# First projection unit in two halves, its first norm's weights fetched ahead of it, in a hybrid transformer layer on one core

## The reference

```python
h = rmsnorm(x, norm_mix[i])
proj = h @ w_in[i]                      # 1024 x 3584
rq, rk, rv, rg, dq, dk, dv = jnp.split(proj, ...)
mix = jnp.concatenate([retention(rq, rk, rv, rg), diff_attention(dq, dk, dv, ...)], axis=-1)
x = x + mix @ w_out[i]
h = rmsnorm(x, norm_ffn[i])
x = x + hierarchical_moe(h, ...)        # 16 experts, two per token
gate = jax.nn.sigmoid(rmsnorm(x, norm_ple[i]) @ w_ple_gate[i])
x = x + gate * (p[i] @ w_ple_proj[i])
return rmsnorm(x, norm_final)
```

## Time and profile before

| what | value |
| --- | --- |
| median of 3 runs | 644.85 us (642.67, 644.85, 647.36) |
| the profiled execution's own time | 644.17 us |
| its span, first to last instruction | 642.3 us |
| mean granted TensorE clock | 0.956 of full speed |
| TensorE busy | 592.3 us, 92% of the span |
| VectorE, ScalarE busy | 33%, 31% |

### The profile page before, as it was taken

How to read it: one execution, slowest core, us unless ns; L and a number is a source line. 1 busy time by engine, 2 the same in 40 slices (tenths; PEclk the granted TensorE clock), 3 DMA queues, 4 the chain that set the end, 5 groups by cost and what they waited for, 6 DMA issues and landing times.

```text
span 642.3 us, 9484 instructions
## 1 busy us (share of the span) xinstructions
PE 592.3 (92%) x3472; PEld 385.3 (60%) x3473; DVE 209.7 (33%) x459; ACT 199.3 (31%) x434; POOL 51.1 (8%) x89
## 2 busy tenths in 40 slices
PE   6999999999999999999879999999999988926994
PEld 5998878878989999985323333333333322305883
DVE  3621264565443352266000111011011100164753
ACT  5532355564543434241300010010010100152774
POOL 0000000000000000001001211212212111110000
PEclk8899999999999999987979999999999999986998
DMA  8743123103210139847596799999999999834001
GB/s 316 198 177 132 66 67 132 65 1 132 67 66 1 66 130 421 353 179 294 213 423 251 285 418 420 421 421 421 420 421 421 420 422 420 345 122 173 33 34 65
DMA packets 47216, 151.52 MB, mean 236 GB/s; under 512 B 7880, under 2 KB 27216, under 8 KB 34640
## 3 DMA queue, kind: packets, MB, share of 16 engines
q1 hardware_dynamic: 43504, 139.77, 55.4%
q0 software_dynamic: 3392, 11.02, 4.4%
q10 hardware_dynamic: 288, 0.29, 0.1%
HBM read 141.62 MB, written 9.45 MB: 235 GB/s over the span
## 4 chain that ended last, share of the span: by engine, by line
PE 81%; DMA 6%; DVE 5%; issue 2%; SPq 2%; ACT 2%; DVEq 0%; ACTq 0%
PE bank L1599 18%; PE bank L1319 13%; PE bank L1320 12%; PE bank L1321 12%; PE bank L1625 10%; DMA ring_dn<-in_w_down 5%; PE bank L1401 2%; PE bank L1526 2%; SPq L579 2%; PE bank L1585 2%; PE bank L1374 2%; DVE ple_lo L1252 2%; DMA gmix<-in_norm_mix 1%; PE bank L1611 1%; PE bank L1415 1%
## 5 line engine op out<-in xcount | busy, mean ns | idle before, releaser
L1599 PE MATMUL bank<-ring_gu,rowsT 128*64 128x512 f32 (+1 forms) x800 | 143.8, 600 | 4.2 <-issue 1.6
L1599 PEld LDWEIGHTS bank<-ring_gu,rowsT 128*64 128x64 f32 (+1 forms) x800 | 43.7, 127 | 89.2 <-issue 85.7
L1625 PE MATMUL bank<-ring_dn,hidT 128*64 128x512 f32 (+1 forms) x400 | 79.1, 631 | 5.6 <-DMA ring_dn<-in_w_down 3.9
L879 ACT ACTIVATE silu_g<-bank 128x256 f32<-128x256 f32 x20 | 7.7, 383 | 218.5 <-PE bank L1599 218.5
L1068 DVE TENSOR_TENSOR w_lo<-w_raw,w_hi 128x2048 fp32r<-128x2048 f32 x18 | 41.3, 2292 | 76.8 <-ACT w_hi L744 69.6
L1218 DVE TENSOR_TENSOR hid<-silu_g,bank 128x256 f32<-128x256 f32 x20 | 8.4, 421 | 150.1 <-ACT silu_g L879 150.1
L1319 PE MATMUL bank<-w_hi,hT_hi 128*128 128x256 f32 x192 | 56.0, 292 | 0.8 <-issue 0.8
L1321 PE MATMUL bank<-w_hi,hT_lo 128*128 128x256 f32 x192 | 54.8, 286 | 0.0
L1320 PE MATMUL bank<-w_lo,hT_hi 128*128 128x256 f32 x192 | 54.8, 286 | 0.0
L1319 PE MATMUL bank<-hT_hi,w_hi 128*128 128x512 f32 x128 | 50.8, 397 | 0.0
L1625 PEld LDWEIGHTS bank<-ring_dn,hidT 128*64 128x64 f32 (+1 forms) x400 | 22.1, 133 | 47.7 <-issue 41.4
(11 more groups left out here) (213 smaller groups left out, 885.4 us busy)
## 6 DMA issues: line engine op xcount, KB each, us to landing
ring_gu<-in_w_gate SPq DMA_DIRECT2D x32, 1024.0 KB
ring_gu<-in_w_up SPq DMA_DIRECT2D x32, 1024.0 KB
ring_dn<-in_w_down SPq DMA_DIRECT2D x16, 2048.0 KB, 22.2
w_raw<-in_w_in SPq DMA_DIRECT2D x14, 1024.0 KB, 4.9
w_raw<-in_w_out SPq DMA_DIRECT2D x4, 1024.0 KB, 4.8
ple_gate_raw<-in_w_ple_gate SPq DMA_DIRECT2D x1, 4096.0 KB, 27.2
yg<-y_rows SPq DMA_DIRECT2D x8, 512.0 KB, 7.4
xr<-in_x SPq DMA_DIRECT2D x4, 512.0 KB, 9.1
```

The lines of the kernel that those rows point to most:

```text
L1599: last = T.matmul(b_gu[q * BLK + t:q * BLK + t + n, :], rowsT[:, k % 4, k // 4, t:t + n], ring_gu[s][:, :, k, q * UC:(q + 1) * UC], start= ...
L1625: last = T.matmul(b_dn[q * BLK + t:q * BLK + t + n, :], hidT[:, kf % 2, kf // 2, t:t + n], ring_dn[s][:, kf, q * (D // 2):(q + 1) * (D // 2)],
```

## The change

SyncE's first transfers come in another order, and unit 0 comes in two halves, by chunks 0 to 3 and 4 to 7 of the input columns: tile 0 of x, `gmix`, first half of unit 0, tile 1, second half, tile 2, tile 3, unit 1. Its splits into high and low parts come in the same halves, on both engines, with the steps of tile 0 moved between them. TensorE does twelve more matmuls on ones after the transposes of tile 0, then the first 12 matmuls of output 0 of unit 0, then the transposes of tile 1, then the other 12. Two new semaphores say that a half of `w_hi` or `w_lo` is there, a third that the first half has landed.

```diff
@@ (SyncE)
             load_x(0)
-            load_unit(0)
             sp.dma_start(gmix[:], norm_mix.rearrange("(o n) -> o n", o=1).to_broadcast([P, D])).then_inc(s_gmix, 16)
-            for i in range(1, NT):
-                load_x(i)
+            for half in range(2):
+                ks = slice(half * KD // 2, (half + 1) * KD // 2)
+                sp.dma_start(w_raw[0][:, ks, :],
+                             w_in_v[:, ks, PARTS[0]:PARTS[0] + UC]).then_inc(s_raw[0] if half else s_half, 16)
+                load_x(half + 1)
+            load_x(3)
             load_unit(1)
@@ (ScalarE)
+            def first_split_hi(half):
+                ks = slice(half * KD // 2, (half + 1) * KD // 2)
+                if half:
+                    act.wait_ge(s_raw[0], 16)
+                else:
+                    act.wait_ge(s_half, 16)
+                return nc.scalar.activation(w_hi[0][:, ks, :], w_raw[0][:, ks, :], ACT.Copy)
+
             x_rms(0)
-            split_hi(0)
+            first_split_hi(0).then_inc(hi_half, 1)
+            h_part(0)
             x_rms(1)
-            h_part(0)
+            first_split_hi(1).then_inc(hi_done, 1)
             x_rms(2)
             h_part(1)
             x_rms(3)
@@ (VectorE)
+            def first_split_lo(half):
+                ks = slice(half * KD // 2, (half + 1) * KD // 2)
+                if half:
+                    dve.wait_ge(hi_done, 1)
+                else:
+                    dve.wait_ge(hi_half, 1)
+                return V.tensor_tensor(w_lo[0][:, ks, :], w_raw[0][:, ks, :], w_hi[0][:, ks, :].bitcast(F32), ALU.subtract)
+
             dve.wait_ge(s_gmix, 16)
             normed(0)
-            split_lo(0)
+            first_split_lo(0).then_inc(lo_half, 1)
+            h_rest(0)
             normed(1)
-            h_rest(0)
+            first_split_lo(1).then_inc(lo_done, 1)
             normed(2)
@@ (TensorE)
+            def first_part(chunks):
+                return three_pass(b_proj[0][:, 0:UC], (hT_hi, hT_lo), (w_hi[0], w_lo[0]), chunks,
+                                  lambda w, k: w[:, k, 0:P], lambda m, k: m[:, k, :])
+
             xn_transpose(0)
+            for n in range(WARM_UP // 2):
+                T.matmul(b_o[:, 0:P], ones[:], ones[:], start=True, stop=True)
+            pe.wait_ge(hi_half, 1)
+            pe.wait_ge(lo_half, 1)
+            pe.wait_ge(h_hi, 1)
+            pe.wait_ge(h_lo, 1)
+            first_part(range(KD // 2))
             xn_transpose(1)
+            pe.wait_ge(hi_done, 1)
+            pe.wait_ge(lo_done, 1)
+            first_part(range(KD // 2, KD)).then_inc(proj_done, 1)
             n_ret = n_mix = 0
             for step, n, *j in schedule():
                 if step == "out":
-                    unit_part(n, *j)
+                    if n or j[0]:
+                        unit_part(n, *j)
```

More of the change, by code:

```diff
@@ L439, in trunk @@
         h_lo = sem("h_lo_ready")
+        hi_half = sem("first_unit_hi_half_ready")
+        lo_half = sem("first_unit_lo_half_ready")
+        s_half = sem("first_unit_half_loaded")
         hi_done = sem("unit_hi_ready")
```

## The result

The changed kernel takes 639.24 us (median of 8 executions, 637.49 to 640.66) against 644.88 (8 executions, 642.67 to 647.36). The ratio is 0.991 with a 95% interval of 0.989 to 0.9929, so it is faster by 0.9%. The forecast was 640.6 in a range of 637.4 to 644.2. The profiled execution took 640.15 us with a span of 638.3, against a forecast of 640.0 and 638.1.

A forecast was written before the change was run, and what follows sets the result against it. TensorE, busy 92% of the span, bounds the kernel; 4.2 us less idle and slow clock at its start gives span 638.1, plus 1.87 outside it and 0.68 to the median: 640.6 us, range 637.4 to 644.2.

The forecast's parts named there:

- The chain and the transfers: Start: transfers land by byte order, `gmix` near 6.8, half 0 at 8.6; output 1 at 17.7, 3.95 us earlier.
- The extra transfer at no cost: Unit 0 as two transfers costs nothing; charged 2.0 us on half 1, the gain would be 3.7 instead of 4.2.
- The clock: TensorE's start: granted clock at 1.00 from 9 to 25 us, so 24 matmuls no longer run at half clock.
- step 4 of the forecast: TensorE's twelve matmuls on ones take 2.6 us, to 12.3, costing nothing at full clock; output 0's first half from 12.45.
- Rival (c): Extra matmuls on ones run at half clock at the start: 3.2 us later than before, 648.0 us; chance 0.03.
- Output 3: Unit 0's output 3 on TensorE starts at 25.1 against 29.35, 4.2 us earlier; bounds 3.0 to 4.9.
- What is behind it: Unit 2 wanted at 39.6, `decay` lands at 34 to 36, earlier slack 4.4 us; the 4.2 us go through.
- The sign that `decay` would no longer be the last thing ahead of unit 2: Expected in the changed profile ahead of unit 2 on TensorE, with unit 2 starting at 39.6.
- The sum: Whole kernel: span 642.3 - 4.2 = 638.1, profiled execution 640.0, median 640.6 us, 0.65% less.
- Rival (a): Gain given back at the clock behind the routing: 644.8 us, expected effect 1.5 us either way; chance 0.10.
- (b): `gmix` lands late at the start, its 128-partition read slower than x: 641.8 us; chance counted within the forecast's 0.80.
- (d): Nothing happens, since something other than `gmix` and the split holds the start: 644.9 us; chance 0.02.

The follow-up runs named there:

- the two edits on top of the change: Changed kernel with ScalarE's evacuation of output 0 ahead of the exponential: 639.36 us; the same plus VectorE's tables wait moved to the first scores: 638.81 and 638.39 us.
- both shifted kernels: Changed kernel with nine or eighteen useless matmuls on ones between units 1 and 2, pushing the rest back: 642.29 and 640.49 us.

## Why the prediction held

**The chain and the transfers.** Right. `gmix` was forecast at 6.8 in bounds of 6.4 to 8.6 and landed at 7.35, half 0 at 8.6 and came at 8.96. Both lay a little later than the marks by bytes. The transposes of tile 0 came at 9.01 (8.90), output 1 at 17.95 (17.7).

**The extra transfer at no cost.** Right for the start: half 1 was not waited for, since ScalarE began its split at 12.47 straight behind the root of tile 1. Unit 1, behind one transfer more and the same bytes, was issued at 4.35 and landed 12.9 us later, at 17.25 against the 16.8 of before. So the extra transfer cost at most 0.45 us there.

```profile
w_raw<-in_w_in SPq DMA_DIRECT2D x1, 1024.0 KB, 12.9
```

The 2.0 us that the Trainium skill (DMA: Bandwidth & Descriptors, Anatomy of one DMA) gives for each DMA, in a section on transfers that GpSimd issues, were not seen as a delay of SyncE's queued ones here.

**The clock.** Right, and it is the part that a reader could have missed. The change keeps TensorE busy from 0.98 on with gaps of at most 0.4 us up to the end of output 2, and the clock is 1.00 throughout. The run without the extra ones shows what step 4 of the forecast costs and buys: the first half of output 0 starts at 12.67 with them and at 12.55 without, and output 3 comes 1.05 us earlier with them. Rival (c), the ones themselves at half clock, came in no run. The nearest is that run, without ones and with the clock down from 12; its output 3 at 26.43 was still 2.9 us ahead of before.

**Output 3.** 4.2 us forecast, 3.97 in the first pair, by the route forecast: `hT_lo` of tile 3 at 23.08 (22.85 forecast) and 2.30 us from there to output 3 (2.29).

**What is behind it.** This step failed in its sizes. I had `decay` land at 34 to 36; it landed at 37.4, 37.9 and 39.1. I took its 8.9 us from issue to landing from a time when one unit and `bias` were ahead of it. Behind both units and `bias` it took 12.2. SyncE's rows, before and then the change, and two windows of the change show the rest:

```profile
22.10 5.50 SPq L541 DMA_DIRECT2D w_raw<-in_w_in  x2
```

```profile
22.07 0.43 SPq L569 DMA_DIRECT2D b_r<-in_b_router_expert  x1
22.62 1.00 SPq L544 DMA_DIRECT2D w_raw<-in_w_in  x2
...
25.25 0.43 SPq L573 DMA_DIRECT2D decay<-const_decay  x1
```

```profile
22.00:24.00 2.00, 2.00 (x19) 2.00 (x18) 2.00 (x3) 1.98 (x3) 0.00 (x0) 1.00 0.29 24
...
26.00:28.00 2.00, 2.00 (x19) 2.00 (x19) 0.00 (x0) 0.00 (x0) 0.00 (x0) 1.00 1.07 366
```

Unit 3 is issued some 4 us earlier, as forecast, and `decay` 3.0 us earlier. But unit 2, first of the 4 MB, is issued no earlier than before (22.62; 22.10, 23.43 and 22.89 in the three profiles of before), because SyncE comes to it only behind the small constants. Its buffer had been free since 15.21, when VectorE's split of the second half ended. The DMA engines are nearly idle from 22 to 24 and full from 26 on. In the three profiles of the change unit 2 is issued at 22.62, 23.01 and 24.09, and `decay` lands 14.8, 14.9 and 15.0 us after that. So by these rows its landing hangs on when SyncE is through with the constants, which the new start does not bring forward. No run moves them. The sign that `decay` would no longer be the last thing ahead of unit 2 did not come. The bound that I gave, "even at 37.15 unchanged, the split is done at 39.44, just in time", was the true state, and with it the slack of 4.4 us was used up to the last 0.1. Two of three profiles fell over that edge, and 0.5 and 1.6 us were lost. That the table is the cause is shown by the two edits on top of the change: without the moved wait nothing is gained, with it unit 2 starts at 38.98 and 38.85, with the table there at 37.8 in the one and only at 39.1 in the other.

**The sum.** The span was forecast at 638.1 and is 638.3. That it is so near is in part luck: the other two profiles of the change have 635.4 and 638.8. The median came out 1.4 us below the forecast. Over all executions the change took 639.4 in the mean (20, standard error 0.3), before 645.1 (76, 0.2): 5.7 us; set by set it is 5.9, 6.0 and 4.4. The markers in three profiles each are at 173.7 and 170.6 in the mean, 3.2 us apart. The remaining 2.5 us lie behind the marker; the same three profiles show 1.4 of them there. Span less marker varies from 465.1 to 468.4 within the changed kernel alone. Windows of 280 to 345 us, of before, the change, and the change again (first repeat):

```profile
280.00:345.00 65.00, 56.90 (x226) 27.72 (x226) 19.51 (x71) 13.68 (x28) 5.68 (x9) 0.84 0.73 286
```

```profile
280.00:345.00 65.00, 57.53 (x216) 25.91 (x216) 17.32 (x66) 12.75 (x24) 6.67 (x10) 0.84 0.76 298
```

```profile
280.00:345.00 65.00, 55.80 (x221) 25.24 (x222) 17.86 (x68) 13.65 (x27) 6.67 (x10) 0.89 0.77 305
```

0.84, 0.84 and 0.89 of full clock there, 0.92 in the third profile of both kernels. Span times twice the clock's shortfall gives the time at 1.2 GHz: 50.6 to 54.7 us in the means of four sets of before, 40.4 to 42.8 in the three sets of the change. The start explains 6.5 of these some 12 us (12.8 to 19.3). The kernel before with ones, whose start is at full clock too, has 43.1, and the change without the extra ones, whose clock falls at 12, has 49.2. So the lower figure goes with a start at full clock rather than with the halves. Rival (a) was named rightly and has come out on the kind side, for which I had left 0.05. Why the clock is kinder later on stays open: neither the moment alone nor the full clock at the start alone fits both shifted kernels. That it is the clock, and not something that goes along with it, is argued from these means, not shown.

**Rivals (b) and (d).** (b) came in a small part: `gmix` landed 0.55 us behind the 6.8 of the forecast, and the matmuls on ones covered all but 0.11 of it. (d) did not come.

## What to carry to other kernels

The first wait in the chain is not the gain. Moving `gmix` alone made the kernel a little slower, since the step behind it then waited on an idle engine with a slower clock; only the halves and the new order, which put each engine's next short step ahead of its next long one, turned the earlier data into an earlier matmul (no run has one of the two without the other). When a start is moved forward by some microseconds, list what was waited for in vain before and how much slack it had, and take a transfer's time to landing with what will then be ahead of it, not with what was. And an effect of half a percent in a kernel whose executions scatter by 0.7% needs several profiles of each side: one pair gave 4.0 us, the means 5.7.

## What the runs showed of the hardware

The clock fell during or just behind gaps that look harmless. In the run without the ones TensorE idled 2.61 us, from 9.9 to 12.55, and the clock was at 0.5 from 12; in before TensorE had idled 2.66 us and worked for 1 us, and the clock was at 0.5 from 12.8 on the earlier trace rows; in the last profile of before it fell near 11.3, within an idle of 3.63 us that ended at 11.91. It came back while TensorE was at work again (by 16 with work from 12.55, at 19.3 with work from 15.06, near 21.5 with work from 15.91). Half of a split took more than half the time: 1.22 us against 2.29 on VectorE, 1.06 against 1.91 on ScalarE.
